# Router logits made per tile inside the output stage instead of at the head of the routing stage

## Chip, core and metric

The kernel runs on one core of one Trainium2 chip. The metric is the device time of one execution in microseconds; lower is better. A core has five engines with a queue each: TensorE (PE; PEld is its weight loads), VectorE (DVE), ScalarE (ACT), GpSimd (POOL) and SyncE (SP), which issues most of the DMAs. Each runs its own instructions in order and waits for the others on semaphores.

## What is computed

Two layers of a trunk over 640 tokens of 1024 features: 128 of a prompt, 512 of a sample. A layer mixes tokens (attention, two recurrent mixers, one output projection, layer norm) and then runs a mixture of 16 experts in which each expert chooses its tokens. The part around the change:

```python
mix = jnp.concatenate([mla_o, hg_o, rw_o], axis=-1) @ p['w_out']
x = _layernorm(DEEPNORM_ALPHA * x + g1 * mix, p['ln_g'][0], p['ln_b'][0])
h2 = x * (1 + sc2) + sh2
# in _expert_choice, for each of the two groups of tokens:
aff = jax.nn.softmax((xf @ router).astype(jnp.float32), axis=-1)   # 16 logits a token
gate, idx = lax.top_k(aff.T, cap)
xe = xf[idx]
```

## The kernel before

The 640 tokens are TILES = 5 tiles of P = 128 tokens, one on each of the 128 partitions; the 1024 features are KD = 8 slices of 128. All is fp32, for which every matmul shows as two records, a transpose as one. e.x holds the residual stream, tokens on partitions. A layer runs as stages (PHASES), each a block of one program for each engine, and a block ends with all engines waiting for each other. Within a stage the order on an engine is the order in which the code is written, and semaphores alone join the engines. Nothing is planned by costs.

phase_output (from L1941). SyncE loads the output weights in two halves (L1963), the norm's rows, then the first expert's weights ahead of need (L2049, L2055), and then stores each finished tile to h2_d in HBM (L1973), from which the experts gather rows; the stage doesn't end before the last store has landed. TensorE makes the product tile by tile (L1985): for a tile two halves of 512 columns, 8 slices each, into two of the 8 PSUM banks; four pairs of banks take turns. norm_steps gives the programs of the others. For each tile VectorE evicts and scales the product (L1895), adds the residual (L1900), takes the statistics (L1902, L1904), ScalarE takes the root (L1921), VectorE the reciprocal (L1883, L1884), ScalarE writes the normalised tile into x (L1923), and GpSimd multiplies and adds the norm's rows (L1930, L1931), after which the tile is final (semaphore n1x). VectorE does tile after tile and waits for ScalarE's root in each.

phase_route (from L2064). TensorE transposes all of x in ten groups of four 128x128 blocks into 8 banks (L2103). ScalarE takes the even groups (L2129) and VectorE the odd ones (L2144); both multiply by the modulation's scale and add its shift on the way to hT, which has room for all tokens. When both are done, TensorE makes the logits, for each tile 8 slices of 128x128 against 16 columns (L2110), into one bank. VectorE copies them (L2148) and starts the softmax; ScalarE does the exponential (L2133) in the middle. Then affinities are turned (L2115), VectorE picks the tokens with max, index and replace steps (L2163 to L2166), and GpSimd issues the first two gathers (L2036). SyncE loads the router weights, the base row and the iota row at the head of the stage (L2084 to L2086).

phase_experts (from L2190) loops over the experts; its first memsets are L2342. phase_norm2 uses norm_steps too.

The central lines of TensorE's program in the old stage:

```python
            pe.wait_ge(S["rx_act"], TILES)
            pe.wait_ge(S["rx_dve"], TILES)
            pe.wait_ge(S["ld_rt"], 48)
            for t in range(TILES):
                for k in range(KD):
                    m = nc.tensor.matmul(ps[:, 0, t * NE:(t + 1) * NE], hT[:, k, t * P:(t + 1) * P], rt[:, k, :],
                                         start=k == 0, stop=k == KD - 1)
```

Of the kernel before, what the change touches and what calls it, by code (L numbers as in the profile page):

```python
# [21 lines left out]
ALU = mybir.AluOpType  # L22
# [3 lines left out]
P = 128  # L26
# [22 lines left out]
ARENA = 40600  # L49
# [1823 lines left out]
def norm_steps(e, pre, src, brow, gb, y, st, src_ready, src_sem, behind):  # L1873
# [44 lines left out]
    def scalar(act):  # L1918
        for t in range(TILES):
# [4 lines left out]
                                 ).then_inc(S[pre + "xn"], 1)  # L1924

# [11 lines left out]
    "n1x", "op_ps", "op_ev", "st_x", "n1ld", "n1var", "n1sd", "n1nm", "n1xn", "ld_wo0", "ld_wo1",  # L1937
# [3 lines left out]
def phase_output(e):  # L1941
# [7 lines left out]
    st, z = e.part(z, TILES, 16)  # L1949
    mem = expert_memory(e)  # L1950
    assert z <= mem["early"]

    def ready(dve, t):
# [3 lines left out]
        e, "n1", lambda t, n: ps[:, 2 * (t % 4) + n, :], brow, gb, y, st, ready, "op_ev", False)  # L1957
    with nc.Block() as block:
        @block.sync
        def _(sp):  # L1960
# [5 lines left out]

            for j in range(4):
                load_w13(e, sp, 0, j, mem)
# [8 lines left out]
        def _(pe):  # L1977
            for t in range(TILES):
                if t >= 4:
                    pe.wait_ge(S["op_ev"], t - 3)  # L1980
                for n in range(2):
                    if t == 0:
                        pe.wait_ge(S[f"ld_wo{n}"], 16)
                    for k in range(KD):
                        m = nc.tensor.matmul(ps[:, 2 * (t % 4) + n, :], e.mixT[:, k, t * P:(t + 1) * P], wo[:, n, k, :],  # L1985
                                             start=k == 0, stop=k == KD - 1)
                    m.then_inc(S["op_ps"], 1)

# [7 lines left out]
        def _(act):  # L1996
            scalar(act)
# [55 lines left out]
def load_w2(e, sp, x, j, mem):  # L2053
# [6 lines left out]
    "ld_rt", "rx_ps", "rx_act", "rx_dve", "lg_ps", "lg_c", "lg_e", "aff", "af_ps", "top", "ti_ps", "iu",  # L2060
# [3 lines left out]
def phase_route(e):  # L2064
# [4 lines left out]
    hT, z = e.part(0, KD, NTOK)  # L2069
    rt, z = e.part(z, KD, NE)  # L2070
    lg, z = e.part(z, TILES, NE)
# [7 lines left out]
    NG = 2 * TILES  # L2079
    with nc.Block() as block:  # L2080
        @block.sync
        def _(sp):
            e.clear_last(sp)
            sp.dma_start(rt, d["router"][l]).then_inc(S["ld_rt"], 16)  # L2084
            sp.dma_start(base, d["base"]).then_inc(S["ld_rt"], 16)
            sp.dma_start(iota, d["iota"]).then_inc(S["ld_rt"], 16)  # L2086
            sp.wait_ge(S["ld_rt"], 48)
# [8 lines left out]
        def _(pe):  # L2096
            for n in range(NG):
                t, b = divmod(n, 2)
                if n >= 8:
                    pe.wait_ge(S["rx_dve" if n % 2 else "rx_act"], (n - 8) // 2 + 1)  # L2100
                for k in range(4):
                    kk = 4 * b + k
                    m = nc.tensor.transpose(ps[:, n % 8, k * P:(k + 1) * P], e.x[:, t, kk * P:(kk + 1) * P], e.ident[:, :])  # L2103
                m.then_inc(S["rx_ps"], 1)
            pe.wait_ge(S["rx_act"], TILES)
# [367 lines left out]
```

## Time and profile before

| | us |
|---|---|
| median of three runs | 3517.41 |
| lowest, highest | 3515.18, 3517.89 |
| profiled execution | 3520.81 |
| its span in the trace | 3519.0 |
| TensorE busy in it | 2804.8 |
| VectorE busy | 1328.5 |
| ScalarE busy | 516.2 |
| GpSimd busy | 692.8 |

The span is the time from the first to the last instruction of the profiled execution; the rest of its time lies around it. The trace's times count from the start of the span. The busy time of an engine is a sum over stages in which different engines set the pace, so what a change is worth is read from the stretch that it touches. That stretch stands twice in the trace: about 967 to 1116 for layer 0, and 2682 to 2830 for layer 1.

### The profile page before, as it was taken

The page shows a single profiled execution, that of the slowest core. Times are in us where ns is not written, and L with a number is a line of the kernel's source. Part 1 is how long each engine was busy: PE and PEld are TensorE (multiplying, and loading weights), DVE is VectorE, ACT ScalarE, POOL GpSimd, SP SyncE. Part 2 cuts the span into 40 slices and gives each one's busy share as a digit, 9 for nine tenths or more (in the row PEclk, how much of TensorE's full clock was granted, in tenths as well). Part 3 has the DMA queues.
Part 4 walks back from the last instruction along what each step waited for, and adds up shares of the span by engine and source line. Part 5 has one row for each costly group of instructions (what it writes and reads, how often), then busy time and mean ns, then how long its engine had stood idle before and what let it go on. Part 6 is the DMA issues. An engine that isn't in the chain of part 4 may idle for free. (4 is left out here: it accounts for less than half of the span.)

```text
span 3519.0 us, 73007 instructions
## 1 busy us (share of the span) xinstructions
PE 2804.8 (80%) x32780; PEld 1886.2 (54%) x32780; DVE 1328.5 (38%) x2741; ACT 516.2 (15%) x987; POOL 692.8 (20%) x844
## 2 busy tenths in 40 slices
PE   5998885638584999999979978564776669999992
PEld 1555554538434666666435645453763456666661
DVE  1101668784624121111250046787654321111215
ACT  0102331131101000100110033302211100010001
POOL 0000908343120000000020054472411100000002
PEclk9999996769886999999989999776897789999996
DMA  8300000000052988898651000000005079898861
GB/s 344 128 19 35 1 9 3 7 1 3 3 215 84 390 336 332 333 346 345 249 244 54 1 35 1 9 3 7 3 2 199 29 273 346 341 351 341 336 245 63
DMA packets 68806, 533.90 MB, mean 152 GB/s; under 512 B 12656, under 2 KB 14512, under 8 KB 32144
## 3 DMA queue, kind: packets, MB, share of 16 engines
q1 hardware_dynamic: 65424, 518.75, 38.0%
q0 software_dynamic: 3072, 10.49, 1.1%
q8 instruction: 259, 4.24, 0.5%
q14 instruction: 51, 0.42, 0.0%
HBM read 520.43 MB, written 8.78 MB: 150 GB/s over the span
## 5 line engine op out<-in xcount | busy, mean ns | idle before, releaser
L2264 PEld LDWEIGHTS ps<-arena 128*64 128x64 f32 x16384 | 579.8, 138 | 102.4 <-issue 99.8
L2264 PE MATMUL ps<-arena 128*64 128x80 f32 x16384 | 600.8, 234 | 29.5 <-DVEq L2363 19.5
L2277 PE MATMUL ps<-arena 128*128 128x512 f32 (+1 forms) x1024 | 469.4, 602 | 5.2 <-ACT arena L2325 4.6
L2386 DVE TENSOR_TENSOR arena<-arena,ps 128x32 f32<-128x32 f32 (+1 forms) x192 | 45.1, 263 | 683.8 <-ACT arena L2333 683.8
L533 PE MATMUL ps<-arena 128*128 128x128 f32 (+1 forms) x1088 | 296.4, 435 | 5.3 <-DVE arena L586 5.3
L2277 PEld LDWEIGHTS ps<-arena 128*128 128x128 f32 (+1 forms) x1024 | 164.0, 169 | 219.8 <-issue 208.9
L2036 POOL DMA_INDIRECT arena<-h_d,arena x32 | 39.8, 1244 | 1015.5 <-DVEq L2357 910.7
L533 PEld LDWEIGHTS ps<-arena 128*128 128x128 f32 x1088 | 164.9, 192 | 137.0 <-issue 131.2
L2368 DVE TENSOR_TENSOR arena<-arena,ps 128x512 f32<-128x512 f32 x160 | 109.9, 687 | 271.1 <-PE ps L2291 214.9
L2333 ACT ACTIVATE arena<-ps 128x160 f32<-128x160 f32 x128 | 38.9, 304 | 942.7 <-PE ps L2264 942.7
L590 DVE COPY arena<-ps 128x128 f32<-128x128 f32 (+3 forms) x48 | 16.3, 340 | 399.4 <-PE ps L533 287.6
L1985 PE MATMUL ps<-arena 128*128 128x512 f32 x320 | 142.9, 610 | 25.6 <-DMA arena<-in_w_out 25.6
L1930 POOL TENSOR_TENSOR x_sb<-x_sb,arena 128x1024 f32<-128x1024 f32 x18 | 43.7, 2429 | 548.6 <-ACT x_sb L1923 548.6
L1118 PE MATMUL ps<-arena 128*128 128x256 f32 x80 | 35.4, 535 | 124.8 <-DVEq L1214 124.8
L435 PE MATMUL ps<-arena,scT 128*2 128x512 f32 x384 | 93.3, 645 | 46.7 <-PEq L341 23.9
L2291 PE MATMUL ps<-arena 128*128 128x512 f32 x256 | 125.2, 615 | 4.3 <-ACT arena L2325 4.3
L539 PE MATMUL ps<-arena 128*128 128x512 f32 (+2 forms) x480 | 125.4, 423 | 0.0
L833 POOL COPY arena<-arena 32x896 f32<-32x896 f32 x2 | 1.9, 925 | 614.6 <-DVE arena L873 614.6
L1985 PEld LDWEIGHTS ps<-arena 128*128 128x128 f32 x320 | 62.6, 196 | 104.6 <-issue 78.7
L539 PEld LDWEIGHTS ps<-arena 128*128 128x128 f32 x480 | 82.0, 189 | 42.8 <-issue 38.5
L890 DVE TENSOR_REDUCE arena<-ps 128x1 f32<-128x768 f32 (+1 forms) x80 | 65.8, 822 | 93.8 <-PE ps L725 87.2
L1109 PEld LDWEIGHTS ps<-arena 128*128 128x128 f32 x560 | 86.2, 231 | 4.5
(331 smaller groups left out, 4071.9 us busy)
## 6 DMA issues: line engine op xcount, KB each, us to landing
arena<-in_ex_w SPq DMA_DIRECT2D x128, 2048.0 KB, 8.5
arena<-in_ex_w SPq DMA_DIRECT2D x128, 1024.0 KB, 7.7
arena<-in_ada_w SPq DMA_DIRECT2D x24, 2048.0 KB, 15.4
arena<-in_w_t SPq DMA_DIRECT2D x34, 512.0 KB, 3.4
arena<-in_w_out SPq DMA_DIRECT2D x4, 2048.0 KB, 10.4
arena<-in_w_tok SPq DMA_DIRECT2D x2, 3712.0 KB, 16.9
h_d<-x_sb SPq DMA_DIRECT2D x10, 512.0 KB, 2.6
arena<-mod_d SPq DMA_DIRECT2D x8, 512.0 KB, 6.6
```

Of the source, the lines that this page charges most:

```text
L435: i = nc.tensor.matmul(ps[PAIR[c], s, :], e.scT[:, k, :], slots[(2 * s + c) % RING][:, k, :], start=k == 0, stop=k == KD - 1)
L533: i = nc.tensor.matmul(ps[:, n % 8, 0:c1 - c0], ring[:, a % WRING, k, :], e.hT[:, k, c0:c1], start=k == 0, stop=k == KD - 1)
L539: i = nc.tensor.matmul(ps[:, n % 8, 0:c1 - c0], e.hT[:, k, a * P:(a + 1) * P], tokw[:, k, c0:c1], start=k == 0, stop=k == KD - 1)
L890: v.link(nc.vector.reduce_max(negm[:, i:i + 1], sc[:, 0:c1 - c0], AX))
L1109: return nc.tensor.matmul(dst, keys, q_level(u, j - 1, hp), start=True, stop=True)
L1930: c.link(nc.gpsimd.tensor_tensor(x[:, t, :], x[:, t, :], gb[:, 0, :], ALU.mult))
L1985: m = nc.tensor.matmul(ps[:, 2 * (t % 4) + n, :], e.mixT[:, k, t * P:(t + 1) * P], wo[:, n, k, :], start=k == 0, stop=k == KD - 1)
L2264: m = nc.tensor.matmul(gated(j)[c * 64:(c + 1) * 64, f, a, :], w13[:, j, a, k, f * P + c * 64:f * P + (c + 1) * 64], xT[:, x % 2, k, :], s ...
L2277: m = nc.tensor.matmul(ps[0:CAP if x % 2 == 0 else P, 4 + h, :], rows[x % 2][:, f, :], w2[:, (f // 2 + 2) % 4, f % 2, h * 512:(h + 1) * 51 ...
L2291: m = nc.tensor.matmul(ps[:, 6 + h, :], GP[:, (t - 1) * P:t * P], yP[:, h * 512:(h + 1) * 512], start=True, stop=True)
L2368: nc.vector.tensor_tensor(yacc[:, t, h * 512:(h + 1) * 512], yacc[:, t, h * 512:(h + 1) * 512], ps[:, 6 + h, :], ALU.add).then_inc(S["sc_e ...
L2386: m = nc.vector.tensor_tensor(rows[b][:, 2 * j:2 * j + 2, to:to + c1 - c0], hs[:, j % 2, :, c0:c1], gated(j)[:, :, 1, c0:c1], ALU.mult)
```

## The change

The product uses two pairs of banks (0 to 3) instead of four. Banks 4 and 5 take the transposes of one tile, and bank 6 the logits of all. TensorE's program in the output stage becomes: products 0, 1, 2, logits 0, products 3, 4, logits 1 to 4. The logits of a tile are 8 transposes of the final tile, a wait for ScalarE, which turns them with scale and shift into hx (room for one tile), and 8 matmuls against the router weights. ScalarE's program gets these turned steps through a new argument after of norm_steps: those of tile t-2 behind the normalisation of tile t, and the last two at the end; each waits for the transposes and for the logits of the tile before. The router weights are loaded in the output stage, ahead of the expert weights. The routing stage loses its transposes, evictions and matmuls and begins with the copy of the logits from bank 6. The arena grows by 1200 floats a partition to hold rt and hx, which moves the expert weights' place by as much. norm_steps in phase_norm2 gets an empty after. A semaphore n1g is allocated and not used.

```diff
-ARENA = 40600
+ARENA = 41800
...
-    def scalar(act):
+    def scalar(act, after):
         for t in range(TILES):
             act.wait_ge(S[pre + "var"], t + 1)
             nc.scalar.activation(st[:, t, 14:15], st[:, t, 13:14], ACT.Sqrt, bias=e.eps[:, 1:2]).then_inc(S[pre + "sd"], 1)
             act.wait_ge(S[pre + "nm"], t + 1)
             nc.scalar.activation(x[:, t, :], y[:, t % 2, :], ACT.Identity, bias=st[:, t, 15:16], scale=st[:, t, 14:15]
                                  ).then_inc(S[pre + "xn"], 1)
+            if t >= 2:
+                after(t - 2)
+        after(TILES - 2)
+        after(TILES - 1)
 
-    "n1x", "op_ps", "op_ev", "st_x", "n1ld", "n1var", "n1sd", "n1nm", "n1xn", "ld_wo0", "ld_wo1",
+    "n1x", "n1g", "ld_rt", "tx_ps", "tx_sb", "lg_ps", "op_ps", "op_ev", "st_x", "n1ld", "n1var", "n1sd", "n1nm", "n1xn", "ld_wo0", "ld_wo1",
...
+    rt, z = e.part(z, KD, NE)
+    hx, z = e.part(z, KD, P)
...
-        e, "n1", lambda t, n: ps[:, 2 * (t % 4) + n, :], brow, gb, y, st, ready, "op_ev", False)
+        e, "n1", lambda t, n: ps[:, 2 * (t % 2) + n, :], brow, gb, y, st, ready, "op_ev", False)
...
             load_norm_rows(e, sp, 0, brow, gb, S["n1ld"])
 
+            sp.dma_start(rt, d["router"][l]).then_inc(S["ld_rt"], 16)
             for j in range(4):
                 load_w13(e, sp, 0, j, mem)
...
         def _(pe):
-            for t in range(TILES):
-                if t >= 4:
-                    pe.wait_ge(S["op_ev"], t - 3)
+            def product(t):
+                if t >= 2:
+                    pe.wait_ge(S["op_ev"], t - 1)
                 for n in range(2):
                     if t == 0:
                         pe.wait_ge(S[f"ld_wo{n}"], 16)
                     for k in range(KD):
-                        m = nc.tensor.matmul(ps[:, 2 * (t % 4) + n, :], e.mixT[:, k, t * P:(t + 1) * P], wo[:, n, k, :],
+                        m = nc.tensor.matmul(ps[:, 2 * (t % 2) + n, :], e.mixT[:, k, t * P:(t + 1) * P], wo[:, n, k, :],
                                              start=k == 0, stop=k == KD - 1)
                     m.then_inc(S["op_ps"], 1)
+
+            def logits(t):
+                pe.wait_ge(S["n1x"], t + 1)
+                if t:
+                    pe.wait_ge(S["tx_sb"], t)
+                for k in range(KD):
+                    m = nc.tensor.transpose(ps[:, 4 + k // 4, (k % 4) * P:(k % 4 + 1) * P], e.x[:, t, k * P:(k + 1) * P], e.ident[:, :])
+                m.then_inc(S["tx_ps"], 1)
+                if t == 0:
+                    pe.wait_ge(S["ld_rt"], 16)
+                pe.wait_ge(S["tx_sb"], t + 1)
+                for k in range(KD):
+                    m = nc.tensor.matmul(ps[:, 6, t * NE:(t + 1) * NE], hx[:, k, :], rt[:, k, :], start=k == 0, stop=k == KD - 1)
+                m.then_inc(S["lg_ps"], 1)
+
+            for t in range(3):
+                product(t)
+            logits(0)
+            for t in range(3, TILES):
+                product(t)
+            for t in range(1, TILES):
+                logits(t)
 
...
-            scalar(act)
+            def turned(t):
+                g = 1 if t else 0
+                act.wait_ge(S["tx_ps"], t + 1)
+                if t:
+                    act.wait_ge(S["lg_ps"], t)
+                for k in range(KD):
+                    m = nc.scalar.activation(hx[:, k, :], ps[:, 4 + k // 4, (k % 4) * P:(k % 4 + 1) * P], ACT.Identity,
+                                             bias=e.modc[:, g, 3, k:k + 1], scale=e.modc[:, g, 4, k:k + 1])
+                m.then_inc(S["tx_sb"], 1)
+
+            scalar(act, turned)
 
...
-    "ld_rt", "rx_ps", "rx_act", "rx_dve", "lg_ps", "lg_c", "lg_e", "aff", "af_ps", "top", "ti_ps", "iu",
+    "ld_ix", "lg_c", "lg_e", "aff", "af_ps", "top", "ti_ps", "iu",
...
-    hT, z = e.part(0, KD, NTOK)
-    rt, z = e.part(z, KD, NE)
-    lg, z = e.part(z, TILES, NE)
+    lg, z = e.part(0, TILES, NE)
...
-            sp.dma_start(rt, d["router"][l]).then_inc(S["ld_rt"], 16)
-            sp.dma_start(base, d["base"]).then_inc(S["ld_rt"], 16)
-            sp.dma_start(iota, d["iota"]).then_inc(S["ld_rt"], 16)
-            sp.wait_ge(S["ld_rt"], 48)
+            sp.dma_start(base, d["base"]).then_inc(S["ld_ix"], 16)
+            sp.dma_start(iota, d["iota"]).then_inc(S["ld_ix"], 16)
+            sp.wait_ge(S["ld_ix"], 32)
 
...
-            for n in range(NG):
-                t, b = divmod(n, 2)
-                if n >= 8:
-                    pe.wait_ge(S["rx_dve" if n % 2 else "rx_act"], (n - 8) // 2 + 1)
-                for k in range(4):
-                    kk = 4 * b + k
-                    m = nc.tensor.transpose(ps[:, n % 8, k * P:(k + 1) * P], e.x[:, t, kk * P:(kk + 1) * P], e.ident[:, :])
-                m.then_inc(S["rx_ps"], 1)
-            pe.wait_ge(S["rx_act"], TILES)
-            pe.wait_ge(S["rx_dve"], TILES)
-            pe.wait_ge(S["ld_rt"], 48)
-            for t in range(TILES):
-                for k in range(KD):
-                    m = nc.tensor.matmul(ps[:, 0, t * NE:(t + 1) * NE], hT[:, k, t * P:(t + 1) * P], rt[:, k, :],
-                                         start=k == 0, stop=k == KD - 1)
-            m.then_inc(S["lg_ps"], 1)
             pe.wait_ge(S["aff"], 1)
             for t in range(TILES):
...
-            for n in range(0, NG, 2):
-                t, b = divmod(n, 2)
-                g = 1 if t else 0
-                act.wait_ge(S["rx_ps"], n + 1)
-                for k in range(4):
-                    kk = 4 * b + k
-                    m = nc.scalar.activation(hT[:, kk, t * P:(t + 1) * P], ps[:, n % 8, k * P:(k + 1) * P], ACT.Identity,
-                                             bias=e.modc[:, g, 3, kk:kk + 1], scale=e.modc[:, g, 4, kk:kk + 1])
-                m.then_inc(S["rx_act"], 1)
             act.wait_ge(S["lg_c"], 1)
...
-            for n in range(1, NG, 2):
-                t, b = divmod(n, 2)
-                g = 1 if t else 0
-                dve.wait_ge(S["rx_ps"], n + 1)
-                for k in range(4):
-                    kk = 4 * b + k
-                    m = nc.vector.tensor_scalar(hT[:, kk, t * P:(t + 1) * P], ps[:, n % 8, k * P:(k + 1) * P],
-                                                e.modc[:, g, 4, kk:kk + 1], e.modc[:, g, 3, kk:kk + 1], ALU.mult, ALU.add)
-                m.then_inc(S["rx_dve"], 1)
-            dve.wait_ge(S["lg_ps"], 1)
-            v.link(nc.vector.tensor_copy(lg, ps[:, 0, 0:TILES * NE].rearrange("p (a b) -> p a b", a=TILES)))
+            v.link(nc.vector.tensor_copy(lg, ps[:, 6, 0:TILES * NE].rearrange("p (a b) -> p a b", a=TILES)))
             m3 = mx.rearrange("p (n o) -> p n o", o=1).to_broadcast([P, TILES, NE])
...
-            scalar(act)
+            scalar(act, lambda t: None)
```

## Rows read from the trace of the kernel before

**Rows 1.** The page: the span, and busy time, share and instructions of TensorE and others

```profile
span 3519.0 us, 73007 instructions
PE 2804.8 (80%) x32780; PEld 1886.2 (54%) x32780; DVE 1328.5 (38%) x2741; ACT 516.2 (15%) x987; POOL 692.8 (20%) x844
```

**Rows 2.** Timeline, layer 0, output stage: start us, us, engine, line, work [idle before <-releaser]

```profile
974.84 71.62 PE L1985 MATMUL ps<-arena 128*128 128x512 f32 x160 [12.81 <-DMA arena<-in_w_out]
...
991.64 1.29 DVE L1895 TENSOR_TENSOR arena<-ps,arena 128x512 f32<-128x512 f32 x2 [32.12 <-PE ps L1985]
...
1019.03 1.29 DVE L1895 TENSOR_TENSOR arena<-ps,arena 128x512 f32<-128x512 f32 x2 [8.68 <-PE ps L1985]
...
1024.18 1.24 ACT L1923 ACTIVATE x_sb<-arena 128x1024 f32<-128x1024 f32 x1 [0.54 <-DVEq L1885]
...
1046.50 1.29 DVE L1895 TENSOR_TENSOR arena<-ps,arena 128x512 f32<-128x512 f32 x2 [8.68 <-PE ps L1985]
```

**Rows 3.** Timeline, layer 0: the last step of the last tile's norm on GpSimd

```profile
1055.38 2.34 POOL L1931 TENSOR_TENSOR x_sb<-x_sb,arena 128x1024 f32<-128x1024 f32 x1
```

**Rows 4.** Timeline, layer 0: the head of the routing stage up to the exponential

```profile
1060.81 6.90 PE L2103 MATMUL ps<-ident_sb,x_sb 128*128 128x128 f32 x40 [14.35 <-PEq L1958]
1061.37 0.33 SPq L2084 DMA_DIRECT2D arena<-in_router  x1
...
1061.94 1.51 ACT L2129 ACTIVATE arena<-ps,modc 128x128 f32<-128x128 f32 x4 [9.05 <-PE ps L2103]
...
1062.79 1.36 DVE L2144 TENSOR_SCALAR arena<-ps,modc 128x128 f32<-128x128 f32 x4 [11.23 <-PE ps L2103]
...
1065.35 4.30 ACT L2129 ACTIVATE arena<-ps,modc 128x128 f32<-128x128 f32 x12 [0.20 <-PE ps L2103]
1069.67 1.28 ACT L2133 ACT_TABLE_LOAD   x1
...
1070.02 15.00 PE L2110 MATMUL ps<-arena 128*128 128x16 f32 x80 [2.31 <-ACT arena L2129]
1085.06 0.24 DVE L2148 COPY arena<-ps 128x80 f32<-128x80 f32 x1 [15.14 <-PE ps L2110]
...
1085.94 0.27 ACT L2133 ACTIVATE arena<-arena 128x80 f32<-128x80 f32 x1 [14.98 <-DVEq L2152]
```

**Rows 5.** Timeline, layer 1: the eviction of tile 4 and the softmax's copy

```profile
2760.30 1.29 DVE L1895 TENSOR_TENSOR arena<-ps,arena 128x512 f32<-128x512 f32 x2 [8.68 <-PE ps L1985]
...
2798.83 0.24 DVE L2148 COPY arena<-ps 128x80 f32<-128x80 f32 x1 [15.28 <-PE ps L2110]
```

**Rows 6.** Windows: us, busy (x instructions) of five queues, granted clock, DMA share, GB/s

```profile
1047.00:1049.00 2.00, 0.00 (x0) 0.00 (x0) 1.85 (x3) 0.00 (x0) 0.00 (x0) 0.89 0.00 0
...
1070.00:1072.00 2.00, 1.98 (x18) 2.00 (x19) 0.00 (x0) 0.96 (x1) 0.00 (x0) 1.00 0.00 0
...
1076.00:1080.00 4.00, 4.00 (x21) 4.00 (x20) 0.00 (x0) 0.00 (x0) 0.00 (x0) 0.50 0.00 0
...
1066.00:1067.70 1.70, 1.70 (x16) 1.47 (x14) 1.00 0.00 0
```

**Rows 7.** Timeline: the last work of three stages and the first of the next

```profile
518.31 2.56 ACT L826 ACTIVATE arena<-ps 128x512 f32<-128x512 f32 x5 [5.37 <-PE ps L770]
521.13 1.28 ACT L1052 ACT_TABLE_LOAD   x1 [0.27 <-PEq L636]
...
1745.61 0.69 DVE L2368 TENSOR_TENSOR arena<-arena,ps 128x512 f32<-128x512 f32 x1 [0.25 <-PE ps L2294]
1746.58 1.28 ACT L1921 ACT_TABLE_LOAD   x1 [12.26 <-PEq L2208]
...
1747.49 1.29 DVE L1895 TENSOR_TENSOR arena<-arena 128x512 f32<-128x512 f32 x2 [1.20 <-SPq L350]
...
1111.30 0.90 POOL L2036 DMA_INDIRECT arena<-h_d,arena  x1 [0.30 <-issue]
...
1116.13 1.09 PEld L2249 LDWEIGHTS ps<-ident_sb,arena 80*128 80x128 f32 x8 [6.88 <-issue]
```

More of the change, by code:

```diff
@@ L2078, in phase_route @@
     assert z <= mem["kept"]
-    NG = 2 * TILES
     with nc.Block() as block:
@@ L2167, in _ @@
             v.link(nc.vector.tensor_copy(pf, pos))
-            dve.wait_ge(S["ld_rt"], 48)
+            dve.wait_ge(S["ld_ix"], 32)
             v.link(nc.vector.tensor_tensor(pf, pf, base, ALU.add))
```

## Prediction

> **What bounds the kernel now.** I read the page first: TensorE is busy for 80% of the span [rows 1], so work taken from its path can count, but the share says nothing of the stretch that the change touches. So I read the timeline of that stretch: in layer 0 from the first output product at 974.84 to the softmax at 1085.06. Two halves have different limits. In the output stage TensorE bounds: five tiles follow without a gap, and the eviction of tile 2 starts at 1019.03, of tile 4 at 1046.50 [rows 2], which is 27.47 / 2 = 13.73 us a tile; VectorE, ScalarE and GpSimd idle for most of each. After 1046.50 everything is one serial chain until the experts. It has three links: the norm of tile 4, with its last GpSimd step starting at 1055.38 and lasting 2.34 [rows 3], then its store and the stage's end; transposes and modulation, 1060.81 to 1070.02; the 80 narrow matmuls, 15.00 us, with the softmax's first copy at 1085.06 behind them [rows 4]. From the last product to that copy that is 38.56 us. Layer 1 has the same: 2798.83 - 2760.30 = 38.53 [rows 5]. So all I need is the new time of that copy, for one layer, times two. The span is 3519.0 us [rows 1], the profiled execution took 3520.81, and the median of the three runs shown is 3517.41, 3.4 lower; I add the change to both.
>
> **Removed.** The whole router front of the second stage: 9.2 us of transposes with two engines evicting, and 15.0 us of matmuls. The norm's tail and the store of tile 4 (14.3 us from 1046.50 to 1060.81) stay, but can now lie beside logits work. TensorE does the same 40 transposes and 80 matmul records; they only move. What is lost is who does the eviction: before, ScalarE and VectorE took 20 steps each in parallel; now ScalarE takes all 40, through one buffer hx of one tile, so that transposes, eviction and matmuls of a tile can't overlap those of the next.
>
> **Banks in two pairs.** Product t now waits for the eviction of tile t-2. Tile 0's starts at 991.64, its two steps take 1.29 (the row of tile 4), and product 2 starts at 1019 - 13.7 = 1005.3 [rows 2]. It has 12 us of cover: cost nothing. The same holds for products 3 and 4.
>
> **The place of logits 0: a stall of TensorE.** TensorE's queue is products 0, 1, 2, logits 0, products 3, 4. Product 2 ends at 1019.0. The eight transposes go at once, but their modulation is queued on ScalarE behind the normalisation of tile 2, the call after(t - 2) at t = 2. That step needs product 2, evicted and normed, and runs from 1024.18 for 1.24, to 1025.42 [rows 2]. So:
> - modulation starts at 1025.45. Eight ScalarE steps: twelve in a row took 4.30 [rows 4], one takes 0.46 by the shape of the four-step rows, so the pitch is (4.30 - 0.46) / 11 = 0.35, and eight take 0.46 + 7 x 0.35 = 2.90. End 1028.35, TensorE resumes 0.1 later, 1028.45 (bounds of that hand-over: 0.04, as from TensorE to the copy, and 0.37, from ScalarE's end at 1069.65 to 1070.02, where VectorE was the later one).
> - the 16 matmuls of a tile. TensorE will have been idle for over 7 us. After the old product 4 the clock began to fall some 2 us behind its last work (0.89 granted in 1047:1049), and the narrow matmuls at the lower level (0.50, 1.2 GHz) ran 21 in 4 us, 0.19 each [rows 6]. 16 x 0.19 = 3.04: end 1031.5. At the full clock they ran 18 in 1.98, 0.11 each, 1.7 in all.
> - product 3 then starts at 1031.5, 12.5 us later than before. What is queued behind the wait is the whole rest of the product.
> - products 3 and 4 take 27.46 at full clock, but start cold. Product 0 did too: 991.64 - 974.84 = 16.80, against 13.73 a tile, less hand-over about 2.9 [rows 2]. I take 2.8; low bound 1.4, half of it, since TensorE has then been at work for 3 us. End of product 4: 1031.5 + 27.5 + 2.8 = 1061.8, against 1046.5: 15.3 us lost.
>
> **The serial tail.** Behind product 4 come logits 1 to 4, one after the other. A round is:
> - eight transposes until ScalarE can start. At half clock ScalarE started 1.13 after the first transpose with four done, VectorE 1.98 after it with eight [rows 4]. At the full clock 16 took 1.70 (the last of [rows 6], which counts L2103 alone), so eight take 0.85 and some 0.4 of latency, 1.3.
> - eight modulation steps, 2.90, and 0.1.
> - sixteen narrow matmuls, 3.04 at half clock, 1.7 at full.
> A cold round is 1.98 + 2.90 + 0.1 + 3.04 = 8.02; a warm one 1.3 + 2.90 + 0.1 + 1.7 = 6.0. In a round TensorE waits 3 us and its 16-column matmuls give it little: in the old stage the clock fell from 1.00 to 0.50 in the midst of 15 us of these very matmuls, without a gap [rows 6]. So I take round 1 with warm transposes, the rest cold: 1.3 + 2.90 + 0.1 + 3.04 = 7.34, and rounds 2 to 4 as 3 x 8.02 = 24.06. End: 1061.8 + 7.3 + 24.1 = 1093.2.
> ScalarE's norm of tile 4 needs its turn between rounds 1 and 2. Its big step starts 5.15 us after the eviction [rows 2], so near 1067, its short root just before; round 1's modulation ends at 1066.0. No collision. GpSimd ends tile 4 some 11.2 us after the product (1055.38 + 2.34 - 1046.50 [rows 3]), at 1073, its store lands by 1076: hidden under rounds 2 and 3, 17 us of cover. Round 4, the first to need it, starts at 1085.
>
> **The boundary.** The logits now end in the stage before, so the copy waits for a stage's end and not for a semaphore. The attention stage's last ScalarE step ended at 520.87 and the next stage began at 521.13: 0.26. After the experts ScalarE started 0.28 after the last VectorE end at 1746.30, VectorE only 1.19 after. After the routing, where GpSimd had just issued two gathers, it was 1116.13 - 1112.20 = 3.9 [rows 7]. TensorE's end is nearest to the first; I take 0.35, bounds 0.26 and 1.19, and 3.9 as a rival. The copy comes at 1093.5. The exponential's table load of 1.28 was hidden behind the matmuls [rows 4]. Now it is the stage's first ScalarE step, as it is at 1746.58 [rows 7], and ends at 1094.75; exponentials used to start 0.88 after the copy, 1094.38. So 0.37 more, up to 1.28 if it is issued after the wait instead.
>
> **Moved transfer.** The router weights' issue, 0.33 on SyncE's queue [rows 4], goes ahead of six expert weight transfers. They are needed some 100 us later, the router's at 1028. Its landing is off the path; so are iota and base. Nothing.
>
> **The sum for a layer.** 1093.5 + 0.37 - 1085.06 = +8.8 us. Layer 1 has the same distances, so +17.6 for both: 3520.81 + 17.6 = 3538.4 for the profiled execution, 3517.41 + 17.6 = 3535.0 against the median. What follows the copy is unchanged: the clock stood at half before the experts either way.
>
> **Where a rule of the notes speaks against a row.** In the old stage transposes alone brought the clock up: the granted clock was 1.00, 2.4 GHz, in 1066:1067.7 [rows 6], with nothing but transposes since 1060.81, the first eight of them at half that pace (0.85 for four [rows 4], against 1.70 for sixteen). The Trainium skill (TensorE: Matmul & The Clock Gate, Part 4: PE-mode transpose) says that transpose-mode work doesn't engage the full clock. The trace does not agree, and by the rule the first rival below would have no chance at all, while the sum would stay. The same page (HAM oscillation — how this bites in real kernels) advises doing work in one dense piece because short bursts parted by waits put the clock down each time; by this rule the cold rounds of 8.02 hold. No row has such bursts with transposes in them.
>
> **Rivals.**
> (1) The clock stays up, and the time is not slower than before. Mechanism: transposes raised the clock once, and four bursts of them, with gaps of 3 us, could hold it. Place: TensorE after product 4. Price: four warm rounds of 6.0 end at 1061.8 + 24 = 1085.8, copy and table 0.7 more: +1.4 a layer, 3517.41 + 2.9 = 3520.3, no measurable change. If product 3 also starts warm, 1.3 + 2.8 us less: -2.8 a layer, 3511.9. It decides from 5.3 us saved of the 8.8 in a layer. For: transposes did it at a full load. Against: they are 0.9 us of each 6 here. Chance 0.06.
> (2) The stall doesn't occur as I read it, because modulation 0 gets to ScalarE before tile 2's norm. Then product 3 starts at 1019.0 + 1.3 + 2.9 + 0.1 + 1.7 = 1025.0, warm; the copy comes 9.3 earlier than forecast and the layer gains 0.5: 3516. Against: one in-order queue, and the diff has the call after the step. Chance 0.02. This is also the case that the change does what it says, logits beside the product.
> (3) The stage's end is dear where TensorE comes last, as at 1116.13: 3.5 more a layer, 3542. Chance 0.07.
> (4) A dearer mixture: the table load after the wait (+0.9), VectorE starting 1.19 late (+0.8), hand-overs of 0.37 (+1.3): +3.0 a layer, 3541. Within my range, chance 0.10.
> The forecast has 0.75.
>
> **How the numbers follow.** Low end of the forecast's own range: half the cold start (-1.4), warm matmuls in round 1 and logits 0 (-2.7): -4.1 a layer, 3527. High end: rivals 3 and 4, 3542. That leaves out rivals 1 and 2, 0.08, and what I haven't thought of. A measurement of this kernel tells about 0.2%, 7 us, from no change: the bounds are 3510.4 and 3524.4. Slower holds the forecast, 3 and 4: 0.90 with a deduction for the unforeseen; same holds rivals 1 and 2: 0.08; faster 0.02.
>
> **What would show it.** In the changed trace: product 3's eviction at about 1048 instead of 1032.8 in layer 0, and TensorE idle 7 us or more after the eighth transpose, ended by ScalarE; the granted clock 0.50 in that gap and in the tail; tile 4's eviction near 1062; four rounds, modulation groups of eight 2.9 us long spaced 8.0; the softmax copy under 0.5 us behind TensorE's last matmul; the copy near 1093.5. Wrong would be: rounds of 6, no gap before product 3, or a copy earlier than 1087.

## The result: slower by 0.66%, and the profile after

| us | before | after |
|---|---|---|
| median | 3517.65 (4 runs, 3515.18 to 3521.21) | 3541.24 (4 runs, 3537.84 to 3544.25) |
| profiled execution's span | 3519.0 | 3542.4 |
| VectorE busy | 1328.5 | 1316.6 |
| ScalarE busy | 516.2 | 529.7 |
| TensorE busy | 2804.8 | 2819.8 |

The ratio is 1.0066, with a 95% interval of 1.0049 to 1.0083. In a second measurement of the changed kernel, against 27 runs of the kernel before, it is 1.0065 (1.0051 to 1.0079). For the second the medians are 3541.01 and 3520.15; their quotient, 1.0059, lies within that interval. The forecast was 3535.0 with a range of 3527 to 3542 and slower at 0.90: the direction held, and the range held by 0.8 us. The size was forecast at 17.6 us and came out at 21 to 24.

The page of the changed kernel, its span and the busy times, beside [rows 1]: the same 32780 matmul records and weight loads, 40 VectorE instructions fewer, 40 ScalarE ones more.

```profile
span 3542.4 us, 73025 instructions
PE 2819.8 (80%) x32780; PEld 1894.8 (53%) x32780; DVE 1316.6 (37%) x2701; ACT 529.7 (15%) x1027; POOL 692.1 (20%) x844
```

The timeline of the changed kernel in layer 0 (start us, us, engine, line, work, idle before and its releaser). L1992 is the product (in the first row products 0 to 2 in one), L2001 the transposes, L2032 ScalarE's modulation, L2007 the logits.

```profile
974.72 43.90 PE L1992 MATMUL ps<-arena 128*128 128x512 f32 x96 [12.82 <-DMA arena<-in_w_out]
...
1018.46 1.04 PE L2001 MATMUL ps<-ident_sb,x_sb 128*128 128x128 f32 x8
1018.66 1.29 DVE L1895 TENSOR_TENSOR arena<-ps,arena 128x512 f32<-128x512 f32 x2 [8.68 <-PE ps L1992]
...
1023.81 1.24 ACT L1923 ACTIVATE x_sb<-arena 128x1024 f32<-128x1024 f32 x1 [0.54 <-DVEq L1885]
1024.95 2.88 ACT L2032 ACTIVATE arena<-ps,modc 128x128 f32<-128x128 f32 x8
...
1027.98 3.57 PE L2007 MATMUL ps<-arena 128*128 128x16 f32 x16 [8.48 <-ACT arena L2032]
1031.38 29.13 PE L1992 MATMUL ps<-arena 128*128 128x512 f32 x64
1046.82 1.29 DVE L1895 TENSOR_TENSOR arena<-ps,arena 128x512 f32<-128x512 f32 x2 [23.11 <-PE ps L1992]
```

The reader is to see one thing first: 8.48 us of idle TensorE in front of L2007, released by ScalarE, while the transposes had been done since 1019.5. Up to 1022.98 ScalarE did nothing: it stood in front of the norm of tile 2, whose root began at 1022.98 and whose big step at 1023.81, and only behind them came the modulation. The eviction of tile 3 is 28.2 us behind that of tile 2; before, it was 13.7 [rows 2].

The tail, same view:

```profile
1060.36 1.04 PE L2001 MATMUL ps<-ident_sb,x_sb 128*128 128x128 f32 x8
1060.56 1.29 DVE L1895 TENSOR_TENSOR arena<-ps,arena 128x512 f32<-128x512 f32 x2 [8.68 <-PE ps L1992]
1061.43 2.90 ACT L2032 ACTIVATE arena<-ps,modc 128x128 f32<-128x128 f32 x8 [8.22 <-PE ps L2001]
...
1064.38 3.08 PE L2007 MATMUL ps<-arena 128*128 128x16 f32 x16 [2.99 <-ACT arena L2032]
...
1067.30 1.95 PE L2001 MATMUL ps<-ident_sb,x_sb 128*128 128x128 f32 x8
...
1075.68 1.95 PE L2001 MATMUL ps<-ident_sb,x_sb 128*128 128x128 f32 x8
1077.66 2.90 ACT L2032 ACTIVATE arena<-ps,modc 128x128 f32<-128x128 f32 x8 [5.47 <-PE ps L2001]
1080.62 3.60 PE L2007 MATMUL ps<-arena 128*128 128x16 f32 x16 [2.99 <-ACT arena L2032]
1084.05 1.95 PE L2001 MATMUL ps<-ident_sb,x_sb 128*128 128x128 f32 x8
...
1088.99 3.60 PE L2007 MATMUL ps<-arena 128*128 128x16 f32 x16 [2.99 <-ACT arena L2032]
1092.87 1.28 ACT L2143 ACT_TABLE_LOAD   x1 [3.94 <-PEq L1964]
1092.91 0.24 DVE L2148 COPY arena<-ps 128x80 f32<-128x80 f32 x1 [27.30 <-PEq L1964]
...
1094.16 0.27 ACT L2143 ACTIVATE arena<-arena 128x80 f32<-128x80 f32 x1
```

Four rounds in which TensorE and ScalarE take turns: each set of logits waits 2.99 us for ScalarE, and in rounds 3 and 4, where ScalarE has nothing else to do, the modulation waits 5.47 us for TensorE. One round is 1084.05 - 1075.68 = 8.37 us. The copy is now released by the stage's end (PEq), not by a matmul, and the table load sits beside it; both answer to [rows 4].

The granted clock is the third number from the right in these windows of the changed kernel, beside [rows 6] (columns as there). The clock is still full in 1022:1024, in the gap, at half in 1024:1028, and at half in the tail.

```profile
1022.00:1024.00 2.00, 0.00 (x0) 0.00 (x0) 1.23 (x5) 0.49 (x2) 0.00 (x0) 1.00 0.00 0
1024.00:1028.00 4.00, 0.02 (x1) 0.06 (x1) 0.00 (x0) 3.83 (x9) 2.80 (x2) 0.50 0.00 0
...
1075.00:1085.00 10.00, 7.01 (x33) 6.61 (x34) 0.00 (x0) 2.90 (x8) 0.00 (x0) 0.50 0.01 2
```

**Where the 23.4 us between the two traces went.** I cut both traces at the first product and at the experts' first transpose, in each layer, and call what lies between the stretch.

| us | before | after | difference |
|---|---|---|---|
| up to the first product, layer 0 | 974.8 | 974.7 | -0.1 |
| stretch, layer 0 | 141.3 | 149.4 | +8.0 |
| experts, layer 0, to the norm behind | 630.4 | 631.6 | +1.2 |
| norm and mixers of layer 1 | 942.4 | 946.8 | +4.5 |
| stretch, layer 1 | 140.7 | 148.9 | +8.2 |
| experts, layer 1, and the end | 689.4 | 691.0 | +1.6 |

16.2 us lie where the forecast put 17.6, and 7.2 where it put none. So there were two questions: are the steps inside the stretch the ones I named, and does something of the change cost outside it?

### The profile page after: what moved, and what is told of

Read it like the earlier page. It is cut to its first block and busy times, and to the rows that moved or that the text cites. A ratio compares the mean times of both kernels' runs of the same rounds, so it can differ in the third digit from the quotient of the medians.

```text
span 3542.4 us, 73025 instructions
## 1 busy us (share of the span) xinstructions
PE 2819.8 (80%) x32780; PEld 1894.8 (53%) x32780; DVE 1316.6 (37%) x2701; ACT 529.7 (15%) x1027; POOL 692.1 (20%) x844
## 5 line engine op out<-in xcount | busy, mean ns | idle before, releaser
L2264 PE MATMUL ps<-arena 128*64 128x80 f32 x16384 | 601.1, 234 | 30.6 <-DVEq L2363 19.5
L2277 PE MATMUL ps<-arena 128*128 128x512 f32 (+1 forms) x1024 | 472.7, 605 | 4.9 <-ACT arena L2325 4.9
L2277 PEld LDWEIGHTS ps<-arena 128*128 128x128 f32 (+1 forms) x1024 | 165.3, 171 | 221.3 <-issue 210.3
L1992 PE MATMUL ps<-arena 128*128 128x512 f32 x320 | 147.3, 624 | 25.5 <-DMA arena<-in_w_out 25.5
L1992 PEld LDWEIGHTS ps<-arena 128*128 128x128 f32 x320 | 63.9, 201 | 106.0 <-issue 80.1
```

The costliest lines, as they stand in the source:

```text
L1992: m = nc.tensor.matmul(ps[:, 2 * (t % 2) + n, :], e.mixT[:, k, t * P:(t + 1) * P], wo[:, n, k, :], start=k == 0, stop=k == KD - 1)
L2264: m = nc.tensor.matmul(gated(j)[c * 64:(c + 1) * 64, f, a, :], w13[:, j, a, k, f * P + c * 64:f * P + (c + 1) * 64], xT[:, x % 2, k, :], s ...
L2277: m = nc.tensor.matmul(ps[0:CAP if x % 2 == 0 else P, 4 + h, :], rows[x % 2][:, f, :], w2[:, (f // 2 + 2) % 4, f % 2, h * 512:(h + 1) * 51 ...
```

## Experiments

The theory was that of the prediction: in each layer a stall of TensorE behind ScalarE's queue, a cold restart, and four serial rounds at half clock. The rivals: other causes inside the stretch (banks, final tiles coming late), and a cost of the moved arena outside. The medians and ratios below compare each kernel with runs of the kernel before that were taken beside it. In this section the stretch is always a layer's, given as layer 0 / layer 1. Three kernels have the unchanged stretch (before, and the two called arena and banks below); its six values lie between 140.4 and 141.3, mean 140.7. Two traces of the changed kernel give 149.4 / 148.9 and 149.6 / 149.6, mean 149.4, so the change costs 8.6 us a layer there.

**The changed kernel again, and the arena alone.** The first is unchanged; the second is the kernel before with this edit:

```diff
-ARENA = 40600
+ARENA = 41800
```

> The changed kernel once more, to size what lies outside the changed stretch. In the two traces the stretch itself (from the first output product to the experts' first transpose) is 8.0 us longer in layer 0 and 8.2 in layer 1, and the rest of the program 7.2 longer. Theory A (the rest is chance from run to run, the change costs the stretch alone): 16 to 18 us over the kernel before, about 3535. Theory B (something of the change also costs elsewhere): 22 to 25 over, about 3541. In either case the stretch is 8 us longer in each layer, to 0.5.

Measured: 3541.01 us against 3520.15 for the kernel before, ratio 1.0065 (1.0051 to 1.0079). The stretch is 8.9 longer than 140.7 in layer 0 and 8.8 in layer 1, where 8 to 0.5 was expected. The rest of the program takes 3238.3 us; in the two traces above it took 3237.0 (before) and 3244.2 (after). So the size was no accident of four runs: the ratio's interval is 18 to 28 us. Theory B, with 22 to 25, fits; theory A, with 16 to 18, touches its lower end at most.

> The kernel before with only the arena grown by 1200 floats, which moves the places of the expert weights and the modulation's weight slots. Theory A: no change, within 3 us of the kernel before, and the stretch as before. Theory B (the moved places cost the 7 us outside the stretch): 3523 to 3526, with the experts' or the modulation's stage longer.

Measured: ratio 0.9998 (0.9989 to 1.0008), stretch 140.7 / 140.6, the rest 3233.6 us. Its theory B falls: the moved places cost nothing. If something costs outside the stretch, it is not the arena; I come back to it below.

**Two pairs of banks alone**, on the kernel before (norm_steps reads the same two pairs):

```diff
...
-                if t >= 4:
-                    pe.wait_ge(S["op_ev"], t - 3)
+                if t >= 2:
+                    pe.wait_ge(S["op_ev"], t - 1)
...
-                        m = nc.tensor.matmul(ps[:, 2 * (t % 4) + n, :], e.mixT[:, k, t * P:(t + 1) * P], wo[:, n, k, :],
+                        m = nc.tensor.matmul(ps[:, 2 * (t % 2) + n, :], e.mixT[:, k, t * P:(t + 1) * P], wo[:, n, k, :],
```

> The kernel before with the product in two pairs of banks instead of four, nothing else. Theory 1 (12 us of cover): evictions stay 13.73 us apart, no change of time. Theory 2 (part of the loss is TensorE waiting for banks): a gap in front of products 2 to 4, and up to 5 us more in a layer.

Measured: ratio 0.9998 (0.9987 to 1.0009), stretch 140.8 / 140.4. Two evictions of its layer 0 timeline, 13.74 apart:

```profile
1023.63 1.29 DVE L1895 TENSOR_TENSOR arena<-ps,arena 128x512 f32<-128x512 f32 x2 [8.68 <-PE ps L1985]
1037.37 1.29 DVE L1895 TENSOR_TENSOR arena<-ps,arena 128x512 f32<-128x512 f32 x2 [8.68 <-PE ps L1985]
```

The banks cost nothing.

**ScalarE's first modulation one tile earlier** in its queue, on the changed kernel:

```diff
-            if t >= 2:
+            if t == 1:
+                after(0)
+            if t >= 3:
                 after(t - 2)
```

> The changed kernel with ScalarE's first modulation steps (tile 0) behind the norm of tile 1 instead of tile 2; TensorE's order is the same. Theory 1 (TensorE stood still because these steps were queued behind tile 2's norm): modulation starts about 1 us after product 2 ends, TensorE's gap before the logits falls from 8.5 to about 3 us, product 3 starts 5 to 6 us earlier, and 10 to 16 us go from the changed kernel's time. Theory 2 (the stall is made by final tiles coming late or by the transposes): the gap stays 8 us and so does the time.

Measured: 3526.96 us, ratio to before 1.0023 (1.0014 to 1.0033), where the changed kernel has 1.0065; stretch 142.9 / 142.7, 6.6 less. Its timeline in layer 0:

```profile
1015.78 1.04 PE L2003 MATMUL ps<-ident_sb,x_sb 128*128 128x128 f32 x8
1016.86 2.90 ACT L2034 ACTIVATE arena<-ps,modc 128x128 f32<-128x128 f32 x8 [8.22 <-PE ps L2003]
1019.90 2.25 PE L2009 MATMUL ps<-arena 128*128 128x16 f32 x16 [3.08 <-ACT arena L2034]
1021.99 29.08 PE L1994 MATMUL ps<-arena 128*128 128x512 f32 x64
```

The gap is 3.08 instead of 8.48 and ScalarE starts 0.04 behind the last transpose. The place of one call in ScalarE's queue is worth 6.6 us a layer; the stall is shown. The logits took 2.25 instead of 3.57, since the clock was still up for most of them (granted 0.84 in 1020:1022), but it stood at 0.50 in 1022:1024, so product 3, which began at 1021.99, restarted cold all the same: products 3 and 4 took 28.9 us in layer 0 and 30.5 in layer 1 instead of 27.5. A wait of 3 us and a tile's narrow matmuls went before it. This order is the one of rival 2, which had priced it at a gain of 0.5 us a layer with a warm restart; the stretch is 2.0 longer than before.

**All products first, rounds still serial**, on the changed kernel. TensorE's order, with ScalarE's steps moved to match:

```diff
-            for t in range(3):
-                product(t)
-            logits(0)
-            for t in range(3, TILES):
+            for t in range(TILES):
                 product(t)
-            for t in range(1, TILES):
+            for t in range(TILES):
                 logits(t)
```

> The changed kernel with all five products first and then five rounds of logits, still one after the other through the one-tile buffer; ScalarE's order is moved to fit. Theory 1 (about 15 us of a layer are the stall and the cold start of product 3, 32 us are four serial rounds): product 4 ends near 1046.4, one round of 7.0 and four of 8.4 follow, the softmax's copy comes near 1087, 2.2 us later than before the change, with the table load 2.5; 5 us for both layers, 3522 to 3525. Theory 2 (the stall is not what costs): the copy stays near 1093, 3535 to 3541.

Measured: 3526.22 us, ratio to before 1.0014 (1.0004 to 1.0023); stretch 142.9 / 142.7. Counted from the first product, the copy came 1.4 us later than before (1084.85 - 973.25 = 111.6 against 110.2), where 2.2 was expected: the first round took 6.2 instead of 7.0. The stall is gone, a fifth round has come, and what is left is still slower than before. Product 3 has no cold restart here (the tail begins 71.4 us after the first product, against 85.6 in the changed kernel), so the serial tail alone gives back all that the overlap with tile 4's norm could win.

**Keeping the clock up in the tail**, on the changed kernel:

```diff
                 m.then_inc(S["tx_ps"], 1)
+                if t:
+                    for i in range(3):
+                        nc.tensor.matmul(ps[:, 7, :], e.mixT[:, i, 0:P], wo[:, 0, i, :], start=True, stop=True)
```

> The changed kernel with three extra 512-column matmuls into an unused bank behind the transposes of rounds 1 to 4, so that TensorE is at work while ScalarE modulates; their results are not read. Theory 1 (2.4 us of each cold round are the lower clock): granted clock 1.00 in the tail, rounds of 5.9 to 6.2 instead of 8.4, the copy 7 to 9 us earlier in a layer, 14 to 18 us off the changed kernel, near 3525. Theory 2 (the pace of a round is ScalarE and hand-overs): the extra work lengthens the rounds or leaves them, 3541 or more.

Measured: 3524.27 us, ratio to before 1.0021 (1.0009 to 1.0034), so 0.44% under the changed kernel; stretch 143.1 / 141.2, 6.3 and 8.2 less. Rounds 3 and 4 in its timeline, with the extra work L2005, and the granted clock over them:

```profile
1066.30 1.07 PE L2001 MATMUL ps<-ident_sb,x_sb 128*128 128x128 f32 x8
1067.20 2.74 PE L2005 MATMUL ps<-arena 128*128 128x512 f32 x6
1067.41 2.91 ACT L2035 ACTIVATE arena<-ps,modc 128x128 f32<-128x128 f32 x8 [3.38 <-PE ps L2001]
1070.37 1.96 PE L2010 MATMUL ps<-arena 128*128 128x16 f32 x16 [0.42 <-ACT arena L2035]
1072.17 1.07 PE L2001 MATMUL ps<-ident_sb,x_sb 128*128 128x128 f32 x8
```

```profile
1064.00:1078.00 14.00, 13.16 (x78) 9.19 (x76) 0.00 (x0) 5.84 (x17) 1.03 (x1) 1.00 0.10 39
```

A round at the full clock is 1072.17 - 1066.30 = 5.87 us, where the prediction had 6.0 for it and the changed kernel has 8.37. So 2.5 us of each cold round are the clock: 0.9 in the transposes (1.95 against 1.07) and 1.6 in the narrow matmuls (3.60 against 1.96). The whole tail, from its first transpose to the copy, took 24.9 us in both layers, one of its rounds cold in part in each (0.50 granted in 1060:1062 in layer 0), against 32.6 and 31.1 in the changed kernel. That layer 0 gained less than layer 1 comes from ahead of the tail: products 3 and 4 took 30.5 us there and 28.9 in layer 1.

**The same in the gap**: eight such matmuls behind the transposes of tile 0 alone.

> The changed kernel with eight extra 512-column matmuls (6.9 us at the full clock) behind the transposes of tile 0, within TensorE's gap of 8.5 us; their results are not read. Theory: clock 1.00 throughout, logits 0 take 2 us instead of 3.4, the eviction of tile 3 comes 15.7 us after product 3's neighbour logits start instead of 18.8, so 3 to 3.5 us off a layer; the gap itself stays, since ScalarE still starts behind the norm of tile 2.

Measured, in one execution (3535.75 us): stretch 147.0 / 146.6, 2.6 less, and not the 3 to 3.5 expected. The logits took 1.93 us, as expected, but products 3 and 4 still took 29.3 us in both layers. The granted clock of three windows in its layer 0:

```profile
1022.00:1024.00 2.00, 1.43 (x13) 1.47 (x14) 0.00 (x0) 0.42 (x2) 1.92 (x2) 1.00 0.03 8
1024.00:1026.00 2.00, 2.00 (x8) 1.04 (x8) 0.00 (x0) 0.00 (x0) 0.49 (x1) 0.85 0.35 143
1026.00:1028.00 2.00, 2.00 (x4) 0.92 (x3) 0.00 (x0) 0.00 (x0) 0.00 (x0) 0.50 0.29 119
```

Product 3 began at 1024.34 at the full clock, which then fell while 512-column matmuls were running: the last 1.6 us of the gap and the 1.9 us of narrow matmuls stood right before. If these were its cause, which no run separates, the cost shows later than its cause.

**The modulation shared with VectorE** for tiles 2 to 4, on the changed kernel: ScalarE's loop ends at slice 4 and TensorE waits for both engines. VectorE gets, behind its norm steps,

```diff
+            for t in range(2, TILES):
+                dve.wait_ge(S["tx_ps"], t + 1)
+                dve.wait_ge(S["lg_ps"], t)
+                for k in range(4, KD):
+                    m = nc.vector.tensor_scalar(hx[:, k, :], ps[:, 4 + k // 4, (k % 4) * P:(k % 4 + 1) * P],
+                                                e.modc[:, 1, 4, k:k + 1], e.modc[:, 1, 3, k:k + 1], ALU.mult, ALU.add)
+                m.then_inc(S["n1g"], 1)
```

> The changed kernel with the modulation of tiles 2, 3 and 4 shared: ScalarE takes slices 0 to 3, VectorE, idle by then, slices 4 to 7. Theory 1 (ScalarE alone, 2.90 us of each serial round): rounds 2 to 4 last 6.9 to 7.1 us instead of 8.4, the copy comes 4 us earlier in a layer, 8 off the changed kernel. Theory 2 (rounds are set by TensorE and hand-overs): rounds stay over 8.

Measured: ratio to before 1.0024 (1.0015 to 1.0034); stretch 145.0 / 145.0, 4.4 less. Two rounds of it:

```profile
1070.68 1.95 PE L2003 MATMUL ps<-ident_sb,x_sb 128*128 128x128 f32 x8
1072.66 1.51 ACT L2043 ACTIVATE arena<-ps,modc 128x128 f32<-128x128 f32 x4 [5.47 <-PE ps L2003]
1072.67 1.36 DVE L2030 TENSOR_SCALAR arena<-ps,modc 128x128 f32<-128x128 f32 x4 [5.61 <-PE ps L2003]
1074.22 3.60 PE L2011 MATMUL ps<-arena 128*128 128x16 f32 x16 [1.60 <-ACT arena L2043]
1077.66 1.95 PE L2003 MATMUL ps<-ident_sb,x_sb 128*128 128x128 f32 x8
```

6.98 us a round, 1.39 less, as the four steps' 1.51 against 2.90 say. So VectorE's absence from the eviction costs 1.4 us in each serial round.

**Two versions that use the idle time.** Both make all products first, put each tile's turned slices into its own place in mixT (no product needs it any more, and the arena stays as before), and use banks 4 and 5 or 2 and 3 in turn, so that transposes and modulation of one tile run beside the logits of another. TensorE's order of pipe behind the products, and what pipe2 changes:

```diff
             turn(0)
             turn(1)
             logits(0)
             turn(2)
             logits(1)
             turn(3)
+            turn(4)
             logits(2)
             logits(3)
-            turn(4)
             logits(4)
```

pipe2 also has, as ScalarE's last step of the output stage:

```diff
+            nc.scalar.activation(st[:, 0, 14:15], st[:, 0, 14:15], ACT.Exp)
```

> A version that makes use of the idle time behind product 4: all five products first, then transposes of a tile into banks 4 and 5 or 2 and 3 in turn while ScalarE modulates the one before, each tile into its own place in mixT, and logits one tile behind; the arena is as before. Tiles 0 to 3 then run beside the norm of tile 4. Theory: TensorE sets the pace, 5.4 us a tile cold, the softmax's copy at 1071 to 1075 instead of 1085.06 in the kernel before, 10 to 14 us off a layer and 20 to 26 off the kernel before. Rival: the modulation on ScalarE alone and the hand-overs keep rounds of 8 us, and the copy stays near 1085.

Measured: 3506.39 us, ratio to before 0.9972 (0.9961 to 0.9983), stretch 132.8 / 132.1, 8.3 less than before. Faster, by less than I had expected (20 to 26 us): tile 4's transposes stood in TensorE's queue behind two sets of logits, though the tile had been final some 10 us earlier, and behind them came a whole serial round of 8.8 us. Besides, two stretches are 16.5 us of gain and the ratio says only 9.8; what is lost outside them is below.

> The pipelined version with the transposes of tile 4 moved ahead of logits 2, where tile 4 has been final for some us, and with a one-column exponential at the end of ScalarE's output stage, so that the table is there before the softmax. Theory: the last round, 8.8 us from its transposes to the copy, loses its transposes and its wait, 4 to 5 us less in a layer of which 1 comes back as a wait for tile 2's place in the banks; the table's 0.4 is gone, and exponentials start 0.9 behind the copy. Copy 3 to 4 us earlier than in the pipelined version, 6 to 9 us off it in all, 16 to 20 below the kernel before. Rival: TensorE's cold narrow matmuls already set the pace and nothing comes but the table's 0.8.

Measured: 3489.03 us, ratio to before 0.9927 (0.9914 to 0.9941), stretch 126.5 / 126.6, 14.2 less than before. Its timeline in layer 0 from the end of the product to the exponential:

```profile
1039.58 1.29 DVE L1895 TENSOR_TENSOR arena<-ps,arena 128x512 f32<-128x512 f32 x2 [8.67 <-PE ps L1992]
...
1052.24 3.24 PE L2006 MATMUL ps<-ident_sb,x_sb 128*128 128x128 f32 x16
1054.22 5.68 ACT L2043 ACTIVATE arena<-ps,modc 128x128 f32<-128x128 f32 x16 [2.69 <-PE ps L2006]
1055.31 4.44 PE L2014 MATMUL ps<-arena 128*128 128x16 f32 x32
1059.92 1.28 ACT L2048 ACT_TABLE_LOAD   x1
1059.96 3.60 PE L2014 MATMUL ps<-arena 128*128 128x16 f32 x16 [0.21 <-ACT arena L2043]
...
1063.88 0.24 DVE L2160 COPY arena<-ps 128x80 f32<-128x80 f32 x1 [19.25 <-PEq L1964]
...
1064.76 0.27 ACT L2155 ACTIVATE arena<-arena 128x80 f32<-128x80 f32 x1 [3.34 <-DVEq L2164]
```

TensorE waits 0.21 us for ScalarE in the last logits, not 2.99; the table load lies beside them, and the exponential starts 0.88 behind the copy, as in the kernel before. The copy comes 24.3 us behind the last eviction's start; before it was 38.6 [rows 2, 4], and 32.4 in the changed kernel. It gained 6 us a layer over pipe, where 3 to 4 were expected: the clock rose during the sixteen transposes in a row (0.50 granted in 1050:1054, 0.77 in 1054:1056, 1.00 in 1056:1058), and the logits behind them took 4.44 us for 32 records, against 6.85 in pipe.

**What is left over outside the stretch.** In the first two traces the rest of the program differs by 7.2 us. Two parts can be placed. In the experts' first gate TensorE starts cold, and the clock rises later than before. Its second 3 us, before and then after (its first 3 us are at 0.50 in both):

```profile
1130.20:1133.20 3.00, 3.00 (x88) 3.00 (x86) 0.00 (x0) 0.00 (x0) 0.00 (x0) 0.95 0.02 5
```

```profile
1138.10:1141.10 3.00, 3.00 (x64) 3.00 (x63) 0.00 (x0) 0.00 (x0) 0.00 (x0) 0.67 0.03 5
```

The first 256 records took 11.43 us instead of 10.62, so 0.8, and 1.6 for both layers. It is no accident of one trace: from the first of these records to the next transposes it is 10.3 to 10.6 us in the six places of the three kernels with the old stretch, and 11.3 to 11.4 in the four of the changed one.

A second place is the last expert of a layer. A run of 32 records there (L2277) takes 13.97 us in all six places of the three kernels with the old stretch, at a granted clock of 1.00, and 15.5 to 15.6 in all four of the changed one, at 0.89 or 0.90, so 1.6 us more in each layer. In layer 0, before and after (the first busy time is TensorE's):

```profile
1718.20:1733.80 15.60, 13.97 (x32) 6.00 (x32) 0.00 (x0) 1.50 (x2) 0.00 (x0) 1.00 1.02 407
```

```profile
1727.30:1742.90 15.60, 15.53 (x32) 6.64 (x32) 0.00 (x0) 0.00 (x0) 0.00 (x0) 0.89 1.02 408
```

The other seven kernels of this study have this dip in seven of their fourteen places, so whether the change brings it about, and how, stays open.

Over both layers, from the experts' first transpose to the norm behind in layer 0 and to the end in layer 1, it is 1317.6 to 1319.8 us in the three kernels with the old stretch, mean 1318.7, and 1322.7 and 1322.8 in the two traces of the changed one: 4.0 more. All nine traces with another stretch lie above all three with the old one (1320.7 to 1328.1). So I take it that what is changed ahead of the experts lengthens them, though their programs are the same; only the two places above are located, other waits in the experts vary too, and why the clock follows the change is open. In pipe it is 3.7 more, which is the larger part of the 6.7 us that its ratio lacks. What lies before the first product and in the mixers of layer 1 shows no such order. The part up to the first product, before the change can act, took 966.1 to 974.8 us over the twelve traces; the RWKV stage of layer 1, up to the issue of the output weights, took 267.6 us in the kernel before and 271.2 in arena. This is where most of the 7.2 us of the first two traces came from, and I take that part for chance. The measured ratio of 1.0065 is 22.9 us on 3520.15, the two stretches are 17.2, the experts 4.0: the remaining 1.7 are within the interval of 18 to 28 us.

## Why the prediction was right, and where its size was off

**Direction and mechanism: right.** From the first product to the copy the prediction had 1093.5 - 974.8 = 118.7 us; it is 118.2 in layer 0 and 118.0 in layer 1. The cost inside the stretch, forecast at 8.8 a layer, is 8.6 on the mean of four. Rivals 1 (clock stays up), 2 (no stall), 3 (a dear stage end) and 4 (the dearer mixture) did not occur. That the sum fits to 0.2 us is in part luck, since terms missed by up to 1.3 us and cancelled, as below. So is the range: its upper end, which the median met to 0.8 us, was set for rivals 3 and 4, and what filled it was a cost in the experts that no term had.

**Banks at no cost:** shown by the run banks.

**The stall, 12.5 us:** product 3 started 1031.38 - 1018.46 = 12.9 us behind the end of product 2, and 56.66 us behind the first product, as forecast. ScalarE ran the modulation right behind tile 2's norm, 2.88 us against 2.90. Shown by the run early.

**Narrow matmuls at 0.19 each, 3.04 a tile: mis-sized.** From the first of them to the next work on TensorE it is 1031.38 - 1027.98 = 3.40 us, and 3.43 in the rounds: 0.21 a record. My 0.19 came from a window row with 21 records in 4 us, but the view also counts the records that a window's edges cut. The stretch of 15.00 us for 80 in [rows 4] would have told better, once the records at the full clock in front are set apart.

**Cold start of product 3, 2.8 us: mis-sized in layer 0.** Products 3 and 4 took 1060.36 - 1031.38 = 28.98 us there, against 27.47 without a gap, so 1.5; in layer 1 it was 30.50, so 3.0. The value was right for one layer, the low bound of 1.4 for the other; in the second trace of the changed kernel both layers have 29.0.

**Rounds of 8.02: 8.37,** nearly all of the difference from the narrow matmuls, and three times 0.35 us in rounds 2 to 4. Round 1 had 7.34 and took 6.94, since the clock was still up for half of its logits; in layer 1 it took 5.84. The split of a cold round between clock and the rest is shown by warm_tail: 5.87 at the full clock, predicted 6.0.

**The boundary:** 0.32 us from TensorE's last end at 1092.59 to the copy, taken at 0.35. **The table load** ended at 1094.15 and the exponential began at 1094.16, 1.25 behind the copy against 0.88 before: 0.37, as forecast.

**The rest of the program at no cost: this is the step that failed,** and it makes up the whole difference between 17.6 and the measured 21 to 24, since the two stretches cost 17.2. I wrote that what follows the copy is unchanged, since the clock stood at half before the experts either way. The level was the same, the moment of its rise was not, and that was worth 1.6 us; with the dip in the last expert and what else differs there, the experts' stages cost 4.0 us.

**Clock and bursts.** The Trainium skill (TensorE: Matmul & The Clock Gate, HAM oscillation — how this bites in real kernels) says that short bursts parted by waits put the clock down again and again; here the trace agrees, with 0.50 granted in 1075:1085, where waits of 3 us stand between bursts of 5.4. That transpose work doesn't engage the full clock, which Part 4 of the same page of the Trainium skill says, does not hold here: in pipe2 sixteen transposes, 3.24 us, stand between narrow matmuls at 0.50 in 1050:1054 and a mean of 0.78 in 1054:1060.

## What to carry to other kernels

Work moved beside other work is only hidden if each engine that it passes through is free at that point of its own queue: look up what stands ahead of the moved step on every engine, not only on the one with the idle time. A batch that two engines share and that streams through eight banks is worth more than its pieces, one behind the other, through one buffer; if it is to be moved early, move the pipeline (a place for each tile, transposes one tile ahead), which here made a loss of 0.66% into a gain of 0.73%. And a pause of TensorE can be paid twice, once as waiting and once as half clock in what follows: here 8.48 us and then 1.5 to 3.0 in the next products.

## What the runs showed of the hardware that I had not expected

The clock fell during dense work: in warm_gap product 3 started at the full clock at 1024.34 and was at 0.50 in 1026:1028, with narrow matmuls and a wait of 1.6 us just before. The cold restart came in two sizes: in the ten places of after, again, early, split and warm_tail products 3 and 4, restarted behind logits 0, took 28.9 to 29.0 us in five and 30.5 or 30.6 in the other five, against 27.5 without a gap; warm_gap, with its extra matmuls, has 29.3. And extra matmuls whose results nobody reads made the program faster by 0.4%, since they held the clock at 1.00 while TensorE would have waited.
